# RWKV quantities of layer 0: token shift as a scaled copy and one product, one inverse for all heads' key norms, exclusive decay read from the inclusive one

## The reference

```python
def rwkv7_mixer(p_b, shift_state, wkv_state, ...):
    prev = jnp.concatenate([shift_state[:, None, :], p_b[:, :-1]], axis=1)
    xs = p_b + (prev - p_b) * b_mu
    r, k, v, wl, al, gl = split_cols(xs, [B_WIDTH, B_WIDTH, B_WIDTH, B_W_LORA, B_A_LORA, B_G_LORA])
    w_log = -jax.nn.softplus(-(b_w0 + jnp.tanh(wl) @ b_w2)) - 0.5
    decay = jnp.exp(-jnp.exp(w_log.astype(f32)))
    a = jax.nn.sigmoid(b_a0 + al @ b_a2)
    g = jax.nn.sigmoid(gl) @ b_g2
    kk = heads(k * b_kk)
    kk = kk * lax.rsqrt(jnp.sum(kk * kk, axis=-1, keepdims=True) + 1e-12)
    k = k * (1.0 + (a - 1.0) * b_ka)
    ...
    bonus = jnp.sum(rh * kh * b_rk, axis=-1, keepdims=True) * vh
    out = ((y + bonus).reshape(b, s, B_WIDTH) * g).astype(p_b.dtype)
```

## Time and profile before

| what | value |
|---|---|
| median of 3 runs | 3897.24 us |
| the profiled execution's own time | 3896.55 us |
| its span in the trace | 3894.8 us |
| TensorE busy | 3111.6 us (80%) |
| VectorE busy | 2702.3 us (69%) |
| ScalarE busy | 1335.9 us (34%) |
| GpSimd busy | 1427.4 us (37%) |
| mean transfer rate | 332 GB/s |
| the block that the change touches | 337.0 to 473.4 us of the span |

### The profile page before, as it was taken

One profiled execution on the slowest core, in us unless ns is written; L12 is line 12 of the kernel. 1 busy time (PEld: TensorE's weight loads), 2 busy tenths in 40 slices (PEclk: granted clock), 3 DMA queues, 4 the chain that ended last, 5 costly groups with the idle time before them and its releaser, 6 DMA issues.

```text
span 3894.8 us, 33849 instructions
## 1 busy us (share of the span) xinstructions
PE 3111.6 (80%) x9394; PEld 1521.5 (39%) x9394; DVE 2702.3 (69%) x6472; ACT 1335.9 (34%) x3949; POOL 1427.4 (37%) x1217
## 2 busy tenths in 40 slices
PE   7866489778877777798989877898898886777777
PEld 4444289643323232244434433333343422322232
DVE  0088645378776666778998857699977667667664
ACT  1134222133333333332557233234552333333332
POOL 0021000045444444455434534454344444444443
PEclk9987599889999999999989999999899999999999
DMA  3100000399999999999989999999999999999998
GB/s 131 34 4 7 0 1 1 118 366 418 416 419 419 420 414 411 415 412 417 392 339 394 396 387 420 419 416 407 354 419 421 421 409 422 421 420 413 415 420 354
DMA packets 210444, 1293.14 MB, mean 332 GB/s; under 512 B 23632, under 2 KB 32848, under 8 KB 62672
## 3 DMA queue, kind: packets, MB, share of 16 engines
q0 software_dynamic: 165888, 1208.03, 75.5%
q1 hardware_dynamic: 44368, 82.96, 5.9%
HBM read 1286.51 MB, written 3.87 MB: 331 GB/s over the span
## 4 chain that ended last, share of the span: by engine, by line
DMA 39%; PE 20%; DVE 10%; issue 7%; ACT 3%; POOL 1%; DVEq 0%; ACTq 0%; POOLq 0%
DMA ring<-in_uv,route 38%; PE banks L1437 14%; DVE ring L1377 4%; DVE X L1387 1%; PE banks L1765 1%; ACT route L1422 1%; POOL ring L1366 1%; PE banks L1825 1%; DVE own L2073 1%; PE banks L1817 1%; ACT route L1407 1%; ACT route L1412 1%; PE banks L1791 1%; DMA own<-in_l_w_out 0%; DMA own<-in_l_peer_wq 0%
## 5 line engine op out<-in xcount | busy, mean ns | idle before, releaser
L1437 PE MATMUL banks<-ring,route 128*128 128x512 f32 (+1 forms) x4088 | 1980.6, 621 | 564.1 <-ACT route L1422 547.1
L1366 POOL DMA_INDIRECT ring<-in_uv,route x1152 | 1330.3, 1155 | 1684.1 <-PE banks L1437 1497.5
L1377 DVE SCALAR_TENSOR_TENSOR ring<-ring,XN 128x1024 f32<-128x1024 f32 x1152 | 1409.7, 1224 | 726.6 <-DMA ring<-in_uv,route 718.1
L1437 PEld LDWEIGHTS banks<-ring,route 128*128 128x128 f32 (+1 forms) x4088 | 723.8, 188 | 1650.7 <-issue 831.3
L1407 ACT ACTIVATE route<-route 128x2 f32<-128x2 f32 x576 | 117.6, 204 | 1868.8 <-DVE ring L1377 1868.4
L1422 ACT ACTIVATE route<-IDN,route 128x128 f32<-128x128 f32 x894 | 309.5, 387 | 4.0 <-PE banks L1437 2.8
L1412 ACT ACTIVATE route<-route 128x1 f32<-128x1 f32 x1152 | 276.9, 287 | 23.7 <-ACT route L1407 0.7
L1765 PE MATMUL banks<-own,QP 128*128 128x512 f32 (+1 forms) x400 | 177.8, 568 | 3.7 <-ACT QP L1856 2.2
L1387 DVE SCALAR_TENSOR_TENSOR X<-ring,route,X 128x1024 f32<-128x1024 f32 x130 | 166.5, 1281 | 0.9
L111 POOL TENSOR_TENSOR ys<-ys,IDN 128x4 f32<-128x4 f32 x9 | 9.1, 1009 | 388.6 <-DVE ys L1114 388.6
L1407 ACT ACT_TABLE_LOAD x106 | 136.0, 1283 | 1.9
(11 more groups left out here) (451 smaller groups left out, 3496.8 us busy)
## 6 DMA issues: line engine op xcount, KB each, us to landing
ring<-in_uv,route POOLq DMA_INDIRECT x1152
own<-in_l_w_in SPq DMA_DIRECT2D x16, 1024.0 KB
own<-in_l_w_out SPq DMA_DIRECT2D x12, 1024.0 KB
own<-in_l_peer_wq SPq DMA_DIRECT2D x12, 1024.0 KB
ring<-in_l_w_in SPq DMA_DIRECT2D x2, 2560.0 KB, 21.6
X<-in_x_prompt SPq DMA_DIRECT2D x8, 512.0 KB, 7.4
ring<-in_l_w_out SPq DMA_DIRECT2D x2, 2048.0 KB, 10.2
ring<-in_l_peer_wq SPq DMA_DIRECT2D x1, 4096.0 KB, 16.0
```

Of the source, the lines that this page charges most:

```text
L1366: pool.indirect_dma_start(self.ring[:, s % RING, :], None, self.io[f"uv{of_slot(s)[0]}"], bass.IndirectOffsetOnAxis(ap=self.EI[:, g % 2, k ...
L1377: dve.scalar_tensor_tensor(u, u, 1.0, self.XN[:, of_slot(s)[1], :], ALU.mult, ALU.mult, accum_out=self.HD[:, g % 2, k:k + 1]).then_inc(sel ...
L1437: m = pe.matmul(self.bank[1 + half][0:n, :], self.DG[:, (V_TENSOR[s] - 1) % 4, 0:n], self.ring[:, s % RING, D + 512 * half:D + 512 * half ...
```

## The change

All of it lies in the block that computes the quantities, but for one transfer.

- Token shift: x + (prev - x) mu becomes (1 - mu) x, a scaled copy on ScalarE (`first`), plus prev mu, one product on VectorE (`shift`). The scales 1 - mu (`omu`) are made at the block's start. The order of the 14 feature tiles is the LoRA inputs 12 and 13, then K of all four pairs, then R and V pair by pair.
- Key norms: ScalarE squares the scaled keys, TensorE sums them per head with 8 columns of marks (`SEL`) into rows of 8 heads for all four pairs, ScalarE takes one root, VectorE one reciprocal (`RIN`, 8 partitions by 576), and TensorE spreads the rows back to each pair (`SELT`, the marks turned); VectorE multiplies the spread out of PSUM.
- Decay: `T4` gets 65 columns per chunk, a first column of ones and the 64 inclusive decays. The exclusive decay is the same tile read one column earlier, so that one subtraction and one exponential per pair go.
- The scaled keys and the rate 1 + (a - 1) ka come from ScalarE.
- The vectors `BV` are loaded once, ahead of the first weights, and kept for both RWKV blocks.

The core of the diff:

```diff
+        BV = sb(lo, "BV", [P, V_MU + BT])
...
+                sp.dma_start(BV[:, :], io["bvec"]).then_inc(bv.h, 16)
...
-        BV, oka = here.take(V_MU + BT), here.take(4)
+        oka, omu, SEL = here.take(4), here.take(BT), here.take(40)
...
-        T4, T5, T0N = (more.take(TOK) for _ in range(3))
+        T4 = more.take(NCH, CHK + 1)
...
+        KN, RIN = PB[:, 12, 0:TOK], PB[0:8, 13, 0:TOK]
+        SELT = PB[0:8, 4, 0:512]
...
+        KF, RF, VF = 4, 0, 8
+        slots = {12: LW, 13: LG}
+        slots |= {KF + p: XS[:, p, :] for p in range(4)}
+        slots |= {RF + p: XS[:, 4 + p % 2, :] for p in range(4)}
+        slots |= {VF + p: XS[:, 6 + p % 2, :] for p in range(4)}
+        mixed = [12, 13, 4, 5, 6, 7] + [f + p for p in range(4) for f in (RF, VF)]
...
-                def shift(slot, ft):
-
-                    x = XS[:, slot, :]
-                    ch.add(dve.tensor_tensor(x[:, 0:SEQ], PB[:, ft, 0:SEQ], PB[:, ft, 1:SEQ + 1], ALU.subtract))
-                    ch(dve.tensor_tensor(x[:, SEQ:], PB[:, ft, SEQ + 1:TOK + 1], PB[:, ft, SEQ + 2:], ALU.subtract))
-                    mu = BV[:, V_MU + ft:V_MU + ft + 1]
-                    ch.add(dve.scalar_tensor_tensor(x[:, 0:SEQ], x[:, 0:SEQ], mu, PB[:, ft, 1:SEQ + 1], ALU.mult, ALU.add))
-                    ch(dve.scalar_tensor_tensor(x[:, SEQ:], x[:, SEQ:], mu, PB[:, ft, SEQ + 2:], ALU.mult, ALU.add))
...
+                def shift(f):
+
+                    x = slots[f]
+                    dve.wait_ge(fs.h, fs.at(2 * mixed.index(f) + 2))
+                    mu = BV[:, V_MU + f:V_MU + f + 1]
+                    ch.add(dve.scalar_tensor_tensor(x[:, 0:SEQ], PB[:, f, 0:SEQ], mu, x[:, 0:SEQ], ALU.mult, ALU.add))
+                    return dve.scalar_tensor_tensor(x[:, SEQ:], PB[:, f, SEQ + 1:TOK + 1], mu, x[:, SEQ:], ALU.mult, ALU.add)
...
+                dve.wait_ge(bv.h, bv.at(16))
+                dve.tensor_scalar(omu, BV[:, V_MU:V_MU + BT], -1.0, 1.0, ALU.mult, ALU.add).then_inc(om.h, 1)
+                dve.tensor_scalar(oka, BV[:, V_KA:V_KA + 4], -1.0, 1.0, ALU.mult, ALU.add).then_inc(om.h, 1)
+                ch(dve.memset(SEL, 0.0))
+                for h in range(2):
+                    dve.tensor_copy(SEL[:, h::10], onesbd[:, 64 * h:64 * h + 1].broadcast_to([P, 4])).then_inc(sl.h, 1)
+                for f in (12, 13):
+                    shift(f).then_inc(sh.h, 1)
...
-                    R, K, V = (XS[:, 3 * (p % 2) + i, :] for i in range(3))
+                    shift(KF + p).then_inc(ks.h, 1)
+                ch.add(shift(RF))
+                ch.add(shift(VF))
+                ch.add(dve.memset(T4[:, :, 0:1], 1.0))
+                dve.wait_ge(zc.h, zc.at(5))
+                for p in range(4):
+                    R, K, V = slots[RF + p], slots[KF + p], slots[VF + p]
                     T0, T3 = T0S[p % 2], T3S[p % 2]
                     dve.wait_ge(zg.h, zg.at(3 * p + 2))
-                    ch(dve.tensor_tensor_scan(T1, scanm, T0, 0.0, ALU.mult, ALU.add))
-                    dve.tensor_tensor(T2, T1, T0, ALU.subtract).then_inc(d1.h, 1)
-                    ahead(0, p + 1)
-                    ahead(1, p + 1)
-                    dve.wait_ge(e1.h, e1.at(3 * p + 3))
-                    ch(dve.tensor_scalar(T1, K, BV[:, V_KK + p:V_KK + p + 1], None, ALU.mult))
-                    dve.tensor_tensor(T2, T1, T1, ALU.mult).then_inc(d2.h, 1)
+                    dve.wait_ge(dve_chain.h, dve_chain.at(ch.n))
+                    dve.tensor_tensor_scan(T1, scanm, T0, 0.0, ALU.mult, ALU.add).then_inc(d1.h, 1)
                     if p == 0:
-                        dve.wait_ge(zc.h, zc.at(5))
-                    blocks(AR[:, :, p, 1, :], R, T4)
-                    ch(dve.tensor_copy(PC[:, :, p], T4[:, 63:TOK:64]))
...
-                        ins = dve.tensor_copy(VB[q, :, 64 * h:64 * h + 64], V[q, :].rearrange("p (c n) -> p c n", c=NCH))
...
-                    dve.wait_ge(rt.h, rt.at(p + 1))
-                    ch(dve.reciprocal(T2, T2))
-                    ch(dve.tensor_tensor(T1, T1, T2, ALU.mult))
-                    blocks(AR[:, :, p, 0, :], T1, T0, -1.0)
-                    ch(dve.tensor_scalar(T2, T3, BV[:, V_KA + p:V_KA + p + 1], oka[:, p:p + 1], ALU.mult, ALU.add))
+                        dve.tensor_copy(VB[q, :, 64 * h:64 * h + 64], chunks(V)[q]).then_inc(vb.h, 1)
+                    if p < 3:
+                        ch.add(shift(RF + p + 1))
+                        ch.add(shift(VF + p + 1))
+                    dve.wait_ge(kt.h, kt.at(2 * p + 1))
+                    dve.wait_ge(bc.h, bc.at(p + 1))
+                    ch.add(dve.tensor_tensor(KN[:, 0:512], KN[:, 0:512], bank[6][:, :], ALU.mult))
+                    ch(dve.tensor_tensor(KN[:, 512:], KN[:, 512:], bank[7][:, 0:64], ALU.mult))
+                    dve.wait_ge(kt.h, kt.at(2 * p + 2))
                     ch.add(dve.tensor_tensor(K, K, T2, ALU.mult))
-                    ch(dve.tensor_tensor(T3, T1, T3, ALU.mult))
-                    blocks(BB[:, :, p, :], T3, T5)
-                    blocks(KB[:, :, p, :], K, T5)
-                    dve.wait_ge(dve_chain.h, dve_chain.at(ch.n))
+                    ch(dve.tensor_tensor(T3, KN, T3, ALU.mult))
+                    dve.wait_ge(e1.h, e1.at(2 * p + 2))
+                    blocks(AR[:, :, p, 0, :], chunks(KN), T4[:, :, 0:CHK], -1.0)
+                    blocks(AR[:, :, p, 1, :], chunks(R), T4[:, :, 1:])
+                    ch.add(dve.tensor_copy(PC[:, :, p], T4[:, :, CHK]))
                     dve.scalar_tensor_tensor(T1, R, BV[:, V_RK + p:V_RK + p + 1], K, ALU.mult, ALU.mult).then_inc(d4.h, 1)
-                    ahead(2, p + 1)
+                    blocks(BB[:, :, p, :], chunks(T3), chunks(T5))
+                    blocks(KB[:, :, p, :], chunks(K), chunks(T5))
                     dve.wait_ge(sp2.h, sp2.at(p + 1))
...
+                def first(f):
+
+                    x, keep = slots[f], omu[:, f:f + 1]
+                    act.activation(x[:, 0:SEQ], PB[:, f, 1:SEQ + 1], ACT.Copy, scale=keep).then_inc(fs.h, 1)
+                    act.activation(x[:, SEQ:], PB[:, f, SEQ + 2:], ACT.Copy, scale=keep).then_inc(fs.h, 1)
...
+                act.wait_ge(om.h, om.at(2))
+                for f in (12, 13, 4, 5):
+                    first(f)
+                act.wait_ge(sh.h, sh.at(2))
+                act.activation(LW[0:64, :], LW[0:64, :], ACT.Tanh).then_inc(tn.h, 1)
+                act.activation(LG, LG, ACT.Sigmoid).then_inc(tn.h, 1)
+                for f in (6, 7):
+                    first(f)
+                for p in range(4):
+                    act.wait_ge(ks.h, ks.at(p + 1))
+                    if p == 0:
+                        act.wait_ge(stt.h, stt.at(1))
+                        act.activation(SELT, bank[7][0:8, :], ACT.Copy).then_inc(stc.h, 1)
+                    if p >= 2:
+                        act.wait_ge(sp1.h, sp1.at(p - 1))
+                    act.activation((KN, T2)[p % 2], slots[KF + p], ACT.Square,
+                                   scale=BV[:, V_KK + p:V_KK + p + 1]).then_inc(d2.h, 1)
+                    if p == 1:
+                        first(RF)
+                        first(VF)
                 lora_out(0)
+                act.wait_ge(sp1.h, sp1.at(4))
+                act.activation(RIN[:, 0:512], bank[6][0:8, :], ACT.Sqrt, bias=eps[0:8])
+                act.activation(RIN[:, 512:], bank[7][0:8, 0:64], ACT.Sqrt, bias=eps[0:8]).then_inc(rt.h, 1)
                 for p in range(4):
+                    if p >= 1:
+                        act.wait_ge(d5.h, d5.at(2 * p))
+                    act.activation(KN, slots[KF + p], ACT.Copy,
+                                   scale=BV[:, V_KK + p:V_KK + p + 1]).then_inc(kt.h, 1)
+                    act.wait_ge(zg.h, zg.at(3 * p + 2))
+                    act.activation(T2, T3S[p % 2], ACT.Identity, bias=oka[:, p:p + 1],
+                                   scale=BV[:, V_KA + p:V_KA + p + 1]).then_inc(kt.h, 1)
                     act.wait_ge(d1.h, d1.at(p + 1))
-                    act.activation(T0S[p % 2], T2, ACT.Exp, scale=-DECAY).then_inc(e1.h, 1)
-                    act.activation(T4[:, :], T1, ACT.Exp, scale=-DECAY).then_inc(e1.h, 1)
-                    act.activation(T5[:, :], T1, ACT.Exp, scale=DECAY).then_inc(e1.h, 1)
-                    act.wait_ge(sp1.h, sp1.at(p + 1))
-                    act.activation(T2[:, 0:512], bank[6][:, :], ACT.Sqrt, bias=eps)
-                    act.activation(T2[:, 512:], bank[7][:, 0:64], ACT.Sqrt, bias=eps).then_inc(rt.h, 1)
+                    act.activation(T4[:, :, 1:], chunks(T1), ACT.Exp, scale=-DECAY).then_inc(e1.h, 1)
+                    act.activation(T5, T1, ACT.Exp, scale=DECAY).then_inc(e1.h, 1)
                     if p + 1 < 4:
+                        first(RF + p + 1)
+                        first(VF + p + 1)
                         lora_out(p + 1)
                     act.wait_ge(vm.h, vm.at(p + 1))
...
+                pe.wait_ge(sl.h, sl.at(2))
```

(20 more changed lines are left out.)

67 lines of the change are left out of this document (30 added, 37 removed).

## The result

The changed kernel takes 3871.76 us (median of 4 runs, 3869.84 to 3877.08) against 3898.19 (4 runs, 3893.45 to 3899.36) of the kernel before on the same chip: a ratio of 0.9937, 95% interval 0.9919 to 0.9954. Run again beside the first experiments it took 3875.4 (5 runs), ratio 0.9944 (0.9930 to 0.9958). It is faster by 22 to 26 us; forecast were 13, with a range of 4 to 27. The profiled execution is the slowest of its four, 3877.08 with a span of 3875.3, so against the profiled one of before it gains 19.5. The traces account for those 19.5; the 3 to 7 us more of the medians lie in executions without a trace and stay open.

What follows compares the result with a forecast made beforehand. VectorE was taken to bound the edited block, which nothing hides. Terms +9.4 + 3.7 - 6.9 - 6.9 - 11.5 = -12.2 us, off the profiled 3896.55, gave 3884.3, forecast 3884; range 3870 to 3893.

Steps and rivals of the forecast that it cites:

- The front: Block start until ScalarE takes the first LoRA products: claimed to end at 364.6, later by 9.4 us.
- The rule drawn from L805: At the block's start: a small one-input VectorE operation waits until the running memset ends; L805 took 3.51 us.
- The copies at 349.6 and 353.5: In the front: VectorE's two four-column copies get through only as successive memsets end, at 349.6 and 353.5.
- Two shifts of 0.9 bring 355.4: In the front: after the copies, VectorE's first two token shifts take 0.9 us each and end at 355.4.
- Pair 0: From the first LoRA products to the first pair's last bonus product: 31.7 us against 28.0, later by 3.7.
- Pairs 1 and 2: Middle pairs: a loop over turned V, ScalarE's chain and two shifts gives a 21.4 us period, 6.9 shorter, twice.
- Pair 3: Last pair, with no next pair to prepare: claimed to take 16.9 us, 11.5 shorter.
- Free gaps: Rival at the block's start: first shifts start near 346 instead of 353.5; 7.8 us more gain, 3876.5; chance 30%.
- Slow TensorE: Rival in the block: TensorE stays at its lower clock, so only 4 us are saved, 3893; chance 13%.
- The rival on the slower side: Chunk stage behind the block: TensorE at 1.2 GHz for 50 us, 22 us lost, net +10, 3907; chance 3%.
- The moved transfer at nothing: Outside the block: loading the vectors earlier costs and gains nothing; without cover, each up to 5.6 us.
- VectorE's count of 34.7 us less work: In the block: VectorE's removed shifts, subtractions, scalings and reciprocals sum to 34.7 us; the path shortens by less.

Runs made afterwards that it cites:

- the first experiments: The earliest follow-up runs on the changed kernel; beside them the unedited changed kernel was run again, at 3875.4 us (5 runs).
- e4_scales_early: Changed kernel, with ScalarE making the scaled R and V copies for pairs 2 and 3 while TensorE turns V; 3871.3 us, ratio to before 0.9920-0.9951.
- e9_warm: Changed kernel plus filler products nobody reads on TensorE around each pair's bonus sums; 3868.1 us, ratio to before 0.9908-0.9941.
- e2_memsets_after: Changed kernel, with GpSimd's memsets waiting until VectorE has made the scalings and marks; 3871.4 us, ratio to before 0.9916-0.9946.
- e10_late_vectors: Changed kernel, with only the vectors' transfer put back behind the block's three LoRA loads; 3879.8 us, ratio to before 0.9937-0.9970.
- quick form: The changed kernel with a front where both scalings pass behind the first memset; block put at 113.1 us, against 116.2 as profiled.
- e5_all: Changed kernel with memsets waiting for VectorE's marks, norms spread before the next LoRA product and ScalarE's next-pair scaled copies earlier; 3854.8 us, ratio 0.9870-0.9903.

## Why the prediction was right, and where it was not

**What bounds.** Right. The block hides nothing, and nothing hides it: 20.1 us of it came off, and 0.5 behind it. The forecast was 12.2 for the block and 3884 for the median; the measured 3871.8 lies close to the low end of the range.

**The front, forecast +9.4, measured +3.1** (start to the end of the first LoRA products: 21.4 us, before 18.2). The rule drawn from L805 was right in kind: small one-input operations wait for memsets, copies too, for which no row of before spoke. Two steps in it failed. "The copies at 349.6 and 353.5": each was to pay for a memset of its own, but both ended with the third, 12.6 us after the start instead of 16.5, 3.9 less. "Two shifts of 0.9 bring 355.4": two-input operations work while the one ahead is held, and ended with it, 1.9 less. The LoRA products at 5.8 instead of 6.4 give the rest. (The forecast's own terms add to 364.5, 9.2 later and not 9.4.) L811 did not get through at 338.0 either, but that cost nothing, since ScalarE waits for L812 too. That the holding costs something was confirmed by taking it away: 9.8 us. The Trainium skill's "SBUF — State Buffer", practical consequences, has copies and scalings take the shared port pair for a whole instruction; the trace agrees for the copies as well (3.84 us for two of 4 columns, 0.24 without a memset beside them).

**Pair 0, forecast +3.7, measured +0.6** (28.6 us from the LoRA products' end, forecast 31.7). The chain was right link for link, its sizes were not: to the root's table load 5.2 instead of 6.6, as the first key sum ran at the faster clock (1.03 us for its 512 columns, forecast 2.3 with its short part); LoRA of pair 1 in 5.9 instead of 6.4; the spread in 1.4 instead of 2.3. All three are TensorE's work, which the clock slowed less than I let it. The reciprocal was 3.74 as assumed, though it has 8 partitions. The table load started 0.02 us behind the end of the activation ahead of it, and the next activation ran 1.29 us later, so the drain that the Trainium skill's "ScalarE: Activation LUTs" adds in its section on what a table load costs is not seen here either.

**Pairs 1 and 2, forecast 21.4, measured 21.76.** The loop is the forecast one: V turned 4.07, V copy, scales, load, exponentials, first of R, two shifts. To the norm product it took 11.6 instead of 11.1, and from there 10.2 instead of 10.3. ScalarE's two scalings took 1.5 instead of 1.2 (392.99 to 394.53), and the first shift began 0.98 behind the start of R's scaled copy (396.99 to 397.97), where I had put 0.7: it waits for both parts of that copy, not for the first alone. e4_scales_early opened the loop and TensorE's arm closed it next; the forecast had that arm at 9.8, and it ends 10.6 us behind the bonus in the change, since its LoRA products take 5.3 and not 4.3. **Pair 3, forecast 16.9, measured 17.73**: "V copy and spread 2.3" took 3.3, as the spread ran at the lower clock (2.07 and 0.52). **The tail**: 4.97 for 5.0.

So of the forecast's -12.2 the loop's -25.3 came as -23.9, and the +13.1 of front and pair 0 as +3.7. The error is theirs, 9.4 us, less 1.4 in the pairs: the sizes of two terms in a mechanism that was there. Both errors went the same way, so nothing made up for them.

**The rivals.** Free gaps (7.8 us more) came in another form: the scalings do pass in six other kernels, and it is worth 3.1 to 3.6, since the copies are then held by the longer memset. Slow TensorE came in pair 3 alone, with the 1.0 us above, although the clock stood at 0.58 over the three pairs; e9_warm prices the slow stretches that the forecast had counted in at some 7.5 us. The rival on the slower side, the chunk stage at the lower clock, exists as a mechanism (0.50 for 24 us behind the block in e2_memsets_after), but cost 4 us and not 22: TensorE was busy for 12.6 of 20 us there, and the clock rose by itself within 28 us of the barrier in every kernel. The moved transfer at nothing was right for the block and for the profiled execution; e10_late_vectors' median leaves it open for the rest.

**What the parts of the change are worth**, by undoing each: the one inverse 11.3, the exclusive decay 0.7 to 1.2, the shift as a scaled copy 1.0. Those make 13 of the quick form's 23, each read from one profiled execution against a reference that is good to 0.5 us; the medians can't tell parts of 1 us. The rest, some 10 us, lies in the squares and scalings moved to ScalarE and the new order; none of these was undone alone, and it is open. VectorE's count of 34.7 us less work (27.6 measured, with the held operations counted as busy) said little about the time, as the forecast warned.

## What to carry to other kernels

Walk the loop, not the sum of an engine's work: 12.6 us taken from the engine with the most work gave 1.0 us, 11.3 us taken where that engine's work stood on the path each time gave 11.3. Such a price holds for the loop in which it was taken: in e5_all, where VectorE waits for less, the new shift may be worth more; that was not tried. When a small one-input VectorE operation stands at the head of a chain beside long GpSimd memsets, let the memsets wait for it: one wait gave 10 us in the block, though alone no fall of the total that is clear of the noise. Then look at the stage behind before counting a gain: TensorE's clock may rise earlier or later there, and between these kernels the entry moved by up to 6 us.

## What was not expected

- A held VectorE operation does not take a gap between two memsets for certain. L811 and L812 lasted 8.65 and 8.58 us, through two memsets, in both profiles of the change, and passed after 0.94 and 0.86 in six other kernels, with the same code on both engines up to there and the same distance to the first memset's start (0.04 us). What decides it is open.
- Two-input operations behind a held copy run in the meantime and end with it: 2.87, 2.20, 2.00, 1.34, 1.15 and 0.49 us for pieces that follow each other.
- A few filler products ahead of the bonus sums took V turned from 4.07 to 2.19 us and the block down by 7.4 to 7.9.
- The clock rises about 5 us behind the block in e4_scales_early and only about 27 us behind it in e2_memsets_after, with the same products in the 24 us ahead of the block's end.
